# Two windowed attentions: GpSimd scales the rows, the sink is a 257th score, mask and maximum are one VectorE operation per head

## What is computed

```python
def neighbourhood_attention(q, k, v, rpb):          # 8 heads, 64 wide; a block of 16 query columns sees 8 x 32 keys
    s = jnp.einsum('brjqhd,brjkhd->bhrjqk', qb, kb).astype(jnp.float32) * (dh ** -0.5)
    s = jnp.where(jnp.asarray(mask), s + bias[None], NEG_INF)
    p = jax.nn.softmax(s, axis=-1).astype(v.dtype)
    o = jnp.einsum('bhrjqk,brjkhd->brjqhd', p, vb)

def swa_sinks(xq, k_sh, v_sh, w_q, b_q, w_o, b_o, sinks):   # 16 heads, 64 wide; a block of 128 queries sees 256 keys
    s = jnp.einsum('bnqkgd,bnskd->bnkgqs', q, kb).astype(jnp.float32) * (ATT_HEAD ** -0.5)
    s = jnp.where(valid[None, :, None, None], s, MASK_VALUE)
    p = jax.nn.softmax(jnp.concatenate([s, sink], axis=-1), axis=-1)[..., :-1]
    o = jnp.einsum('bnkgqs,bnskd->bnqkgd', p.astype(vb.dtype), vb)
```

## Time and profile before

| what | value |
|---|---|
| time, median of 3 runs | 3261.55 us (3259.87 to 3263.14) |
| the profiled execution's own time | 3250.07 us |
| its span, first to last instruction | 3248.3 us |
| TensorE busy (matmul) | 3037.7 us, 94% of the span |
| weight loads of TensorE | 2441.5 us, 75% |
| GpSimd busy | 1170.4 us, 36% |
| VectorE busy | 1073.4 us, 33% |
| ScalarE busy | 965.3 us, 30% |

### The profile page before, as it was taken

How to read it: one execution, slowest core, us unless ns; L and a number is a source line. 1 busy time by engine, 2 the same in 40 slices (tenths; PEclk the granted TensorE clock), 3 DMA queues, 4 the chain that set the end, 5 groups by cost and what they waited for, 6 DMA issues and landing times.

```text
span 3248.3 us, 49144 instructions
## 1 busy us (share of the span) xinstructions
PE 3037.7 (94%) x20792; PEld 2441.5 (75%) x20792; DVE 1073.4 (33%) x1481; ACT 965.3 (30%) x1206; POOL 1170.4 (36%) x331
## 2 busy tenths in 40 slices
PE   8979999999999967999998899998999997899998
PEld 6748778887888845778887688886888865678886
DVE  4451242223211165234442421126211147541212
ACT  3153232223222246322221322223212235531222
POOL 4303343343443432322221344434444440234344
PEclk9999999999999978989998999999999999999999
DMA  4202222222222212331101122222222220122222
GB/s 183 91 6 99 91 78 100 95 91 91 91 96 99 91 52 117 134 111 46 42 26 35 55 100 91 96 98 78 91 91 104 91 81 27 41 77 97 95 92 78
DMA packets 42571, 271.82 MB, mean 84 GB/s; under 512 B 4736, under 2 KB 4864, under 8 KB 12704
## 3 DMA queue, kind: packets, MB, share of 16 engines
q1 hardware_dynamic: 39312, 252.64, 22.0%
q10 hardware_dynamic: 3088, 16.65, 1.3%
HBM read 254.58 MB, written 14.68 MB: 83 GB/s over the span
## 4 chain that ended last, share of the span: by engine, by line
issue 60%; PE 19%; POOL 15%; DVE 4%; DVEq 1%; ACT 1%; POOLq 0%; DMA 0%; ACTq 0%
POOL w_lo L469 15%; PE ps L750 8%; PE ps L578 3%; PE ps L580 2%; PE ps L579 2%; PE ps L665 1%; DVE small L1545 1%; POOL x_res L546 1%; DVEq L1544 1%; DVE work L1404 0%; PE ps L672 0%; DVE work L1487 0%; DVE ybuf L1560 0%; DVEq L1484 0%; PE ps L762 0%
## 5 line engine op out<-in xcount | busy, mean ns | idle before, releaser
L469 POOL TENSOR_TENSOR w_lo<-w_raw,w_hi 128x2048 fp32r<-128x2048 f32 x220 | 1023.8, 4654 | 1734.3 <-ACT w_hi L983 1725.3
L578 PE MATMUL ps<-act_hi,w_hi 128*128 128x512 f32 x2240 | 893.7, 399 | 44.2 <-DVE act_lo L1432 23.6
L579 PE MATMUL ps<-act_lo,w_hi 128*128 128x512 f32 x2240 | 887.7, 396 | 0.0
L580 PE MATMUL ps<-act_hi,w_lo 128*128 128x512 f32 x2240 | 887.5, 396 | 0.0
L983 ACT CAST w_hi<-w_raw 128x2048 fp32r<-128x2048 f32 x219 | 417.3, 1905 | 1039.7 <-PE ps L580 1015.6
L578 PEld LDWEIGHTS ps<-act_hi,w_hi 128*128 128x128 f32 x2240 | 424.6, 190 | 157.0 <-POOL w_lo L469 27.7
L579 PEld LDWEIGHTS ps<-act_lo,w_hi 128*128 128x128 f32 x2240 | 424.5, 190 | 99.2 <-issue 1.7
L580 PEld LDWEIGHTS ps<-act_hi,w_lo 128*128 128x128 f32 x2240 | 424.4, 189 | 99.3
L578 PE MATMUL ps<-hid_hi,w_hi 128*128 128x512 f32 x1184 | 472.1, 399 | 24.8 <-POOL w_lo L469 15.3
L580 PE MATMUL ps<-hid_hi,w_lo 128*128 128x512 f32 x1184 | 469.8, 397 | 0.0
L579 PE MATMUL ps<-hid_lo,w_hi 128*128 128x512 f32 x1184 | 469.5, 397 | 0.0
(11 more groups left out here) (251 smaller groups left out, 2389.8 us busy)
## 6 DMA issues: line engine op xcount, KB each, us to landing
w_raw<-stream SPq DMA_DIRECT2D x224, 1024.0 KB, 4.8
spill<-work ACTq DMA_DIRECT2D x5, 2048.0 KB, 6.3
scratch<-spill SPq DMA_DIRECT2D x24, 256.0 KB, 4.1
work<-bias_in SPq DMA_DIRECT2D x1, 3072.0 KB, 18.9
work<-spill SPq DMA_DIRECT2D x12, 256.0 KB, 3.1
x_res<-x_in SPq DMA_DIRECT2D x2, 1024.0 KB, 8.1
spill<-area ACTq DMA_DIRECT2D x4, 512.0 KB, 5.3
area<-spill SPq DMA_DIRECT2D x7, 256.0 KB, 2.8
```

What stands on the lines that cost most here:

```text
L469: tt(w_lo[:, s, :], w_raw[:, s, :], w_hi[:, s, :].bitcast(F32), ALU.subtract).then_inc(S["lo_made"], 1)
L578: mm(out, wh, hi[:, k, :], start=(k == 0) if begin is None else begin, stop=False)
L579: mm(out, wh, lo[:, k, :], start=False, stop=False)
L580: return mm(out, wl, hi[:, k, :], start=False, stop=end)
```

## The change

- GpSimd's program gets `softmax(a)`: it scales the rows of P of each step (one `tensor_scalar` a head), and in attention 0 it gathers the block of v. VectorE keeps the reciprocal and signals it with a new semaphore, `at_recip`.
- The mask's addition and the maximum are one `tensor_tensor_reduce` a head. A new semaphore, `at_added`, frees the scores' banks for TensorE; `at_max` still follows the negation.
- In attention 1 P has 257 columns. TensorE writes the sink into column 256 of the four score banks (a product of one column a head, in the two of every four steps that come first); the mask's table has a zero there; the exponential and its sum run over 257. The separate operations on sinks are gone.
- `p_buf` has four buffers in place of three, and the lags differ. TensorE's iteration t: scores(t), for t under 4 a product of no use in both attentions, transposes of v and of P of step t-3, output(t-4). ScalarE's iteration t: exponential(t), copy of v and copy of P of step t-3, output copy(t-5).
- ScalarE runs a one-column exponential ahead of each attention (`preload`).

```diff
--- before.py
+++ after.py
...
     ok = (s - 128 <= q) & (s > q)
-    return np.stack([np.where(ok & (s >= 128), 0, MASKED), np.where(ok, 0, MASKED)], 1).astype(np.float32)
+    table = np.zeros((P, 2, 257), np.float32)
+    table[:, :, 0:256] = np.stack([np.where(ok & (s >= 128), 0, MASKED), np.where(ok, 0, MASKED)], 1)
+    return table
...
-        p_buf = yflat[:, 1536:3072].rearrange("p (b h k) -> p b h k", b=3, h=2)
-        pt_buf = yflat[:, 3072:4096].rearrange("p (b h a k) -> p b h a k", b=2, h=2, a=2)
+        p_buf = yflat[:, 0:2056].rearrange("p (b h k) -> p b h k", b=4, h=2)
+        pt_buf = yflat[:, 2056:3080].rearrange("p (b h a k) -> p b h a k", b=2, h=2, a=2)
+        swa_mask = work[:, 18:20, :].rearrange("p k t -> p (k t)")[:, 0:514].rearrange("p (b k) -> p b k", b=2)
+        NEG_MAX, SUM, MAX, RECIP = 12, 16, 20, 24
+        KEYS = (256, 257)
+
+        def tiny(at, t, count=2):
+            return small[:, at + 2 * (t % count):at + 2 * (t % count) + 2]
...
+            def softmax(a):
+
+                g0, steps = 16 * a, STEPS[a]
+                for t in range(steps):
+                    if a == 0:
+                        tile, j = divmod(t, 4)
+                        if t >= 2:
+                            pool.wait_ge(S["at_vt"], t - 1)
+                        v = work[:, 8 + tile, :].rearrange("p (r c) -> p r c", c=64)[:, :, NA_KEY0[j]:NA_KEY0[j] + 32]
+                        nc.gpsimd.tensor_copy(vb_buf[:, t % 2, :].rearrange("p (r c) -> p r c", c=32), v).then_inc(S["at_vblk"], 1)
+                    pool.wait_ge(S["at_recip"], g0 + t + 1)
+                    for h in range(2):
+                        p = p_buf[:, t % 4, h, 0:256]
+                        inst = nc.gpsimd.tensor_scalar(p, p, tiny(RECIP, t, 4)[:, h:h + 1], None, ALU.mult)
+                    inst.then_inc(S["at_p"], 1)
+
             lo(0, 0)
-            done = 1
+            split(1, FIRST["conv_branch"] + 1)
+            pool.wait_ge(banks_free[1], 6)
+            softmax(0)
...
+                if name == "mixer1_post":
+                    split(done, FIRST["o2"] + 1)
+                    softmax(1)
+                    done = FIRST["o2"] + 1
...
             def attention(a, q_of, k_of, v_of):
                 g0, steps = 16 * a, STEPS[a]
-                for t in range(steps + 3):
-                    if a == 1 and t == 2:
+                for t in range(steps + 4):
+                    if a == 1 and t == 3:
                         pe.wait_ge(banks_free[1], FIRST["o2"] // 2)
                     if t < steps:
                         if t >= 2:
-                            pe.wait_ge(S["at_max"], g0 + t - 1)
+                            pe.wait_ge(S["at_added"], g0 + t - 1)
                         for h in range(2):
+                            out = ps[:, SCORE_BANKS[t % 2] + h, :]
+                            if a == 1 and t % 4 < 2:
+                                mm(out[:, 256:257], c("ident"), sinks[:, 2 * (t // 4) + h:2 * (t // 4) + h + 1], start=True, stop=True)
                             for part, keys in enumerate(k_of(t, h)):
                                 n = 256 // len(k_of(t, h))
-                                inst = mm(ps[:, SCORE_BANKS[t % 2] + h, n * part:n * part + n], q_of(t, h), keys, start=True, stop=True)
+                                inst = mm(out[:, n * part:n * part + n], q_of(t, h), keys, start=True, stop=True)
                         inst.then_inc(S["at_s"], 1)
-                        if a == 1 and t < 3:
-                            stay_warm(1, bank=5)
-                    if a == 0 and 1 <= t <= steps:
-                        u = t - 1
-                        if u:
-                            pe.wait_ge(S["at_vtok"], u)
-                        pe.wait_ge(S["at_vblk"], u + 1)
-                        for part in range(2):
-                            inst = nc.tensor.transpose(ps[:, 5, 128 * part:128 * part + 128],
-                                                       vb_buf[:, u % 2, 128 * part:128 * part + 128], c("ident"))
-                        inst.then_inc(S["at_vt"], 1)
-                    if 2 <= t <= steps + 1:
-                        u = t - 2
+                        if t < 4:
+                            stay_warm(1, bank=5 if a else 4)
+                    if 3 <= t <= steps + 2:
+                        u = t - 3
+                        if a == 0:
+                            if u:
+                                pe.wait_ge(S["at_vtok"], u)
+                            pe.wait_ge(S["at_vblk"], u + 1)
+                            for part in range(2):
+                                inst = nc.tensor.transpose(ps[:, 5, 128 * part:128 * part + 128],
+                                                           vb_buf[:, u % 2, 128 * part:128 * part + 128], c("ident"))
+                            inst.then_inc(S["at_vt"], 1)
                         pe.wait_ge(S["at_p"], g0 + u + 1)
                         if u >= 2:
                             pe.wait_ge(S["at_ptsb"], g0 + u - 1)
                         for h in range(2):
                             for part in range(2):
                                 inst = nc.tensor.transpose(ps[:, TURN_BANKS[u % 2], 256 * h + 128 * part:256 * h + 128 * part + 128],
-                                                           p_buf[:, u % 3, h, 128 * part:128 * part + 128], c("ident"))
+                                                           p_buf[:, u % 4, h, 128 * part:128 * part + 128], c("ident"))
                         inst.then_inc(S["at_pt"], 1)
-                    if t >= 3:
-                        u = t - 3
+                    if t >= 4:
+                        u = t - 4
                         pe.wait_ge(S["at_ptsb"], g0 + u + 1)
+                        if a == 0:
+                            pe.wait_ge(S["at_vtok"], u + 1)
                         if u:
                             pe.wait_ge(S["at_osb"], g0 + u)
-                        elif a == 0:
-                            pe.wait_ge(S["at_vtok"], u + 1)
                         for h in range(2):
                             for part in range(2):
...
             def attention(a):
+
                 g0, steps = 16 * a, STEPS[a]
-                for t in range(steps + 3):
-                    if a == 0 and 1 <= t <= steps:
-                        u = t - 1
-                        tile, j = divmod(u, 4)
-                        if u >= 2:
-                            act.wait_ge(S["at_vt"], u - 1)
-                        v = work[:, 8 + tile, :].rearrange("p (r c) -> p r c", c=64)[:, :, NA_KEY0[j]:NA_KEY0[j] + 32]
-                        nc.scalar.copy(vb_buf[:, u % 2, :].rearrange("p (r c) -> p r c", c=32), v).then_inc(S["at_vblk"], 1)
+                for t in range(steps + 5):
                     if t < steps:
-                        g, b, e = g0 + t, t % 3, t % 2
-                        act.wait_ge(S["at_max"], g + 1)
+                        act.wait_ge(S["at_max"], g0 + t + 1)
+                        if t >= 2:
+                            act.wait_ge(S["at_recip"], g0 + t - 1)
                         for h in range(2):
-                            inst = af(p_buf[:, b, h, :], p_buf[:, b, h, :], ACT.Exp,
-                                      bias=small[:, 12 + 2 * e + h:13 + 2 * e + h],
-                                      accum_out=small[:, 16 + 2 * e + h:17 + 2 * e + h])
-                        if a == 1:
-                            for h in range(2):
-                                inst = af(small[:, 24 + 2 * e + h:25 + 2 * e + h],
-                                          sinks[:, 2 * (t // 4) + h:2 * (t // 4) + h + 1], ACT.Exp,
-                                          bias=small[:, 12 + 2 * e + h:13 + 2 * e + h])
+                            p = p_buf[:, t % 4, h, 0:KEYS[a]]
+                            inst = af(p, p, ACT.Exp, bias=tiny(NEG_MAX, t)[:, h:h + 1], accum_out=tiny(SUM, t)[:, h:h + 1])
                         inst.then_inc(S["at_exp"], 1)
-                    if a == 0 and 1 <= t <= steps:
-                        u = t - 1
+                    if a == 0 and 3 <= t <= steps + 2:
+                        u = t - 3
                         act.wait_ge(S["at_vt"], u + 1)
                         if u >= 2:
                             act.wait_ge(S["at_o"], u - 1)
                         nc.scalar.copy(vt_buf[:, u % 2, :, :], ps[:, 5, 0:256].rearrange("p (a k) -> p a k", a=2)).then_inc(S["at_vtok"], 1)
-                    if 2 <= t <= steps + 1:
-                        u = t - 2
+                    if 3 <= t <= steps + 2:
+                        u = t - 3
                         act.wait_ge(S["at_pt"], g0 + u + 1)
                         if u >= 2:
                             act.wait_ge(S["at_o"], g0 + u - 1)
                         nc.scalar.copy(pt_buf[:, u % 2, :, :, :],
```

(49 more changed lines are left out.)

5 lines of the change are left out of this document (3 added, 2 removed).

## The result

| | time, median | ratio to the kernel before | attention 0 | attention 1 |
|---|---|---|---|---|
| before | 3260.71 us (4 runs) | | 57.47 us | 96.18 us |
| after | 3379.40 us (3372.35 to 3381.38, 4 runs) | 1.0361 [1.0343, 1.0379] | 80.85 | 191.79 |

The changed kernel is 118.7 us slower, 41 us above the predicted time and 7 above the upper end of its range. They grew by 23.4 and 95.6 us, together 119.0: the loss lies in the two attentions. The rest of the profiled execution grew by 3.3 us, which is less than it varies between kernels that don't differ there (see the end of the experiments).

A forecast was written before the change was run, and what follows sets the result against it. The prediction took a one-step ring through the engines, closed by ScalarE's late output copy, as the bound. Attention 1 +50, attention 0 +15 and clock +11 gave +76 us, a median of 3338, range 3306 to 3372.

The forecast's parts named there:

- The ring: Both attentions: scores, mask, exponential, copies, output product close over one step; 4.77 us with sinks in attention 1, 4.71 in 0.
- signs of the mechanism: Changed timeline: TensorE waits some 2.5 us for ScalarE's output copy, VectorE for scores, ScalarE for the negation, never together.
- signs of size: Scores starts 4.5 to 5.3 us apart in attention 1; windows about 146 to 157 us and 73 to 78.
- a time above 3372: Rival: something in the ring is far dearer, the combined pair above 1.5 us or GpSimd scaling above 2.3; chance 0.10.
- pair of combined operations: VectorE's mask addition and maximum for both heads, up to the negation: 1.05 us, bounds 0.75 and 1.5.
- GpSimd scaling: Each of two scalings a step on GpSimd takes 0.6 us, 0.43 to 0.71, covered by the step.
- Its terms at full clock: Attention 1's ring links, 0.59, 0.83, 1.05, 0.20, 1.00, 0.46 and 0.41, together 4.54 us without sinks.
- The clock: Half of the 36 ring steps at 1.2 GHz, 0.6 us more each: +11 us, bounds 0 and +22.
- ring steps: Steps from the second output product on: 26 of 31 in attention 1, 10 of 15 in attention 0.
- The sinks: Attention 1: two one-column products, 0.46 us in half of the steps, 0.23 on average, lower bound zero.
- First steps and tail: Outside the ring: first steps 10 us in attention 1, 12 in 0; from the last scores on 12.4 and 13.4.
- slack ring: Rival: output copy(t-5) is ready in time, TensorE bounds; 13 us less in attention 1, 14 in 0, 3235; chance 0.05.

The follow-up runs named there:

- e1: The changed kernel with the output copy moved from the end of ScalarE's iteration to its start: 3234.05 us.
- e5: The changed kernel with the outputs of attention 1 alternating between banks 3 and 5, ScalarE's order untouched: 3270.85 us.
- b1: The kernel before with the output copy made one iteration later (t-4 in place of t-3), behind exponential(t), in attention 1 alone: 3360.64 us.
- e4: The changed kernel with two products of no use (128x512) ahead of each output product in attention 1: 3343.69 us.
- e7: The changed kernel with the output copy first in ScalarE's iteration and both sink products ahead of both heads' scores: 3223.75 us.
- e9: e7 with the scaling back on VectorE, GpSimd only gathering v in attention 0: 3216.33 us.

## Why the prediction was right about the mechanism and low in its size

**The ring: right.** The prediction had it close over one step from the second output product on, through output copy(t-5) behind exponential(t). e1 and e5 cut it at two places, and b1 built it in the old kernel. The signs of the mechanism that it named are there: TensorE's wait of 2.40 us ended by the output copy, VectorE waiting for scores, ScalarE for the negation. The signs of size are missed: steps of 5.30 and 7.43 us where 4.5 to 5.3 was named, and windows of 191.79 and 80.85 us where at most 157 and 78 was. The prediction gave 0.10 to a time above 3372, for a pair of combined operations over 1.5 us or a GpSimd scaling over 2.3; these took 0.88 and 0.92, so the time lies there for other reasons, the clock and the sinks.

**Its terms at full clock: right.** Forecast 4.54 us for a plain step of attention 1, measured 4.32 (e4). One of the changed kernel's own steps in attention 1 also has it, 4.32 us between negations, where the others have 5.30. The pair of combined operations to the negation is 0.88 us in place of 1.05: a second one starts 0.35 us after the first, though each is 0.43 long. That is 0.17 of the 0.22.

**The clock: mis-sized most.** The prediction took half of the 36 ring steps at 1.2 GHz and 0.6 us for each, 10.8 us; the upper end of its range had all of them, still at 0.6. Attention 1 ran 25 of 26 ring steps at half clock, and each cost 0.98: 24.5 us in place of 7.8. The sinks cost 0.90 us more in each of their 12 steps at half clock than at full (2.13 and 1.23), another 10.8 us that had no term. In attention 0 every second step was at half clock, as forecast, at 0.99 in place of 0.6. The 0.6 came from the earlier trace rows, a scores product of 1.03 us in the first steps of attention 0, taken for one at half clock, where in the ring it takes 1.23. It was not at half clock throughout. Window of the kernel before over that product, where the clock was 0.50 from 180.00 to 182.00 and 1.00 behind it:

```profile
181.69:182.72 1.03, 1.03 (x5) 0.51 (x4) 0.87 (x5) 0.65 (x3) 0.00 (x0) 0.66 0.00 0
```

The clock rose while it ran, which the trace of before showed. The Trainium skill (TensorE: Matmul & The Clock Gate, HAM oscillation) has the clock falling again and again in such patterns; attention 0 does that, while attention 1 fell once and stayed down but for a step. Why the two differ the runs don't show.

**The sinks: mis-sized.** Forecast 0.46 us in each step that has them, by one-column products that stand among their like the earlier trace rows, with a lower bound and no upper one. Measured 2.13, in 12 of the 26 ring steps: 25.6 us in place of 6.0, of which 10.8 are the clock's. The two products themselves were priced nearly right, 0.54 us at full clock (e7). The step that failed is that only the new instructions were priced, and not what they do to their neighbours: another 0.71 us at full clock, 1.19 at half. The earlier trace rows already had a hint: eight records of scores (L702) take 0.72 us, hardly more than four of a transpose (L722, 0.66). The Trainium skill (TensorE: Matmul & The Clock Gate, Part 3: Packing small matmuls) says that small products on different tiles of the array run concurrently. The kernel after agrees: 1.23 us for both heads, 1.22 for one.

**First steps and tail: low.** Outside the ring steps attention 1 took 29.4 us (forecast 22.4), attention 0 30.2 (25.4). The last outputs of attention 1 came 3.1 us apart in place of 2.12, at half clock, which the sum had left out there.

The account of the profiled execution, forecast 3326, measured 3372.35:

| term | forecast | measured | difference |
|---|---|---|---|
| attention 1, 26 plain steps at full clock | 118.0 | 112.3 | -5.7 |
| their half clock | 7.8 | 24.5 | +16.7 |
| its sinks, at full clock (1.23, e4) | 6.0 | 14.8 | +8.8 |
| half clock on the sinks | none | 10.8 | +10.8 |
| its first steps and tail | 22.4 | 29.4 | +7.0 |
| attention 0, 10 ring steps with clock | 50.1 | 50.7 | +0.6 |
| its first steps and tail | 25.4 | 30.2 | +4.8 |
| all else | 3096.2 | 3099.7 | +3.5 |

**GpSimd: wrong in size, right in place.** A scaling took 0.92 us, outside the 0.43 to 0.71 of the prediction. At 1.82 us a step nobody waited for it in the ring of 4.6 us and more. With the ring gone next to nobody waits for it either (0.4 us in e7), and it is no gain (e9).

**The rival "slack ring"** gave 3235 for a kernel in which output copy(t-5) is not behind exponential(t). e1 is that kernel: 3234.05. The agreement is partly luck: sink steps cost more than it assumed, attention 0 gained its 13 us (forecast 14), attention 1 gained 6 (forecast 13), and the other 5 us of the 24 lie outside the attentions.
